# Convolution inputs by one 512-column product per weight tile, with the rounded and leftover halves of the rows side by side

## The chip, the cores and the metric

The kernel runs on one core of a Trainium2 chip as one program. The time is device microseconds of that core for one execution, from a few executions; lower is better. The engines are named as the profile names them: PE (TensorE; PEld are its weight loads, which overlap the matmuls), DVE (VectorE), ACT (ScalarE), POOL (GpSimd) and SP, which here only starts DMAs.

## The reference, cut to what matters

Two blocks of two layers each work on a sequence of 256 rows and 1024 features, all in float32. The change touches the second block, where each layer makes 2048 convolution channels from the normed rows `u` (256 x 1024):

```
z = u @ w_in                                   # its first 2048 columns are m_qk
m_qk = silu(causal_dwconv(m_qk, m_conv_w, m_conv_b))
# y[t] = w[3]*x[t] + w[2]*x[t-1] + w[1]*x[t-2] + w[0]*x[t-3] + b, for each channel
m_q, m_k = split(m_qk, 2)                      # 4 heads of 256 each; mlstm_chunkwise uses them
```

Beside it each of these layers has a sliding-window attention with 16 query heads, an mLSTM with 4 heads, two gates, and two feed-forward parts.

## The kernel before, in words

**Products.** A float32 product is made of three products in PE's `float32r` type. Each operand is split into a rounded part and what is left of it: `wh` and `wl` for weights, `xh` and `xl` for the normed and transposed rows (`[128, 8, 256]`: 8 feature tiles `kt` of 256 sequence positions). The kernel adds high x high, low x high and high x low in PSUM. Weights come in 778 units of 128 x 1024 values. SP loads a unit into `raw` (a ring of 11), ACT rounds it into `wh` (L1250, ring of 8), and DVE subtracts to make `wl` (L1475, ring of 11).

**Forms.** In the form "rows" (L1918 to L1926) a 128 x 128 tile of `xh` or `xl` is loaded into the array and 512 weight columns stream past it. In the form "features" (L1906 to L1916), which only the convolution uses, the weight tile is loaded and the 256 positions stream past it, so that channels lie on the partitions. A convolution chunk has 256 channels: two units of 4 `kt` each and two channel tiles `ct`, each into columns 0 to 255 of its own PSUM bank. That is 48 matmuls of 256 columns. Each layer has 8 chunks, so 16 chunks in all.

**After the product.** For each `ct`, ACT writes `w[3]*x + b` from the bank into `mT` (L1352), and DVE then adds the three shifted taps from the bank in place (L1711: 255, 254 and 253 columns), each waiting for the one before it. The last one frees the bank (`d_done`). A later step `conv_silu` lets ACT take a tanh (L1357) and DVE finish the silu (L1719). The matmuls that read `mT` come much later (L2026, L2027).

**Order.** All engines walk one list of steps, each in order. `weave` mixes the dense units with the side work by a table written by hand (`UNITS_AMONG_2` here). The side work between the convolution chunks is the attention. For a pair of heads, PE makes scores (L2049, L2052), DVE masks them and takes the maximum (L1806 to L1819), ACT takes the exponential (L1431, L1434), DVE makes reciprocals of the sums (L1561, L1563), ACT scales the probabilities `Pn` (L1262, semaphore `evened`), PE transposes them (L1979), ACT copies them to `PT` (L1314), and PE multiplies by the values (L2064, L2066). The chunks are numbered 0 to 7 below. Chunk 3 of each layer stands on DVE directly ahead of L1561 and L1563, as does chunk 4, and PE's next transposes wait for the `evened` that follows.

Of the kernel before, what the change touches and what calls it, by code (L numbers as in the profile page):

```python
# [8 lines left out]
F32R = mybir.dt.float32r  # L9
I32 = mybir.dt.int32  # L10
ALU = mybir.AluOpType
ACT = mybir.ActivationFunctionType
# [3 lines left out]
P = 128  # L16
S = 256
R = S // P
D = 1024
KT = D // P  # L20
# [562 lines left out]
def plan_block2(p, t_x):  # L583
# [27 lines left out]
    def convolved(i, pair):  # L611
        c = p.chunk(("w_in", [(256 * i, 256 * i + 256)]), "x", KT, 256, pair, t_x, form="features")
        p.add("conv", c=c, i=i, n=p.count("tapped", 2) - 2)
        q["conv", i] = c

    q = {}
# [20 lines left out]
    def silu(i):  # L637
        p.add("conv_silu", i=i, c=q["conv", i], n=p.count("conv"))

# [101 lines left out]
    for j in range(2):  # L741
# [5 lines left out]
        c = Step("chunk", u=u, pair=1, nth=nth)  # L747
# [114 lines left out]
def build(nc, plan, a):  # L862

    with ExitStack() as ctx:
        def sem(name):
            return ctx.enter_context(nc.semaphore(name))
# [44 lines left out]
        spread_out = sem("spread_out")  # L911
        tapped = sem("tapped")
        conv_tanh = sem("conv_tanh")
        floored = sem("floored")
# [24 lines left out]
        o = 0  # L939
        raw, end = mem.at("raw", o, [P, NR, UNIT])  # L940
        wl, o = mem.at("wl", o, [P, NR, UNIT], F32R)
        wh, o = mem.at("wh", o, [P, NH, UNIT], F32R)
        xh, o = mem.at("xh", o, [P, KT, S], F32R)
        xl, o = mem.at("xl", o, [P, KT, S], F32R)
        x, o = mem.at("x", o, [P, R, D])
# [6 lines left out]
        b = {}  # L952
# [31 lines left out]
        for n in ("dq", "dk", "dv"):  # L984
# [61 lines left out]

        split_of = {"x": (xh, xl), "oa": (b["oa_h"], b["oa_l"]), "ob": (b["ob_h"], b["ob_l"]),
                    "oc": (b["oc_h"], b["oc_l"]), "act": (b["act_h"], b["act_l"]), "hm": (b["hm_h"], b["hm_l"]),
# [16 lines left out]
        with nc.Block() as block:  # L1065
# [168 lines left out]
            def _(act):  # L1234
# [8 lines left out]
                for st in steps:  # L1243
# [102 lines left out]
                    elif k == "conv":  # L1346
                        act.wait_ge(unit_done, st.c.u + 1)
                        act.wait_ge(p_conv, 16 * (st.l + 1))
                        for ct in range(2):
                            c = 2 * st.i + ct  # L1350
                            w = b["convw"][:, c, :]
                            act.activation(b["mT"][:, c, :], DB[2 * st.c.pair + ct][:, 0:S], ACT.Identity,  # L1352
                                           scale=w[:, 3:4], bias=w[:, 4:5]).then_inc(tapped, 1)
                    elif k == "conv_silu":
                        for ct in range(2):
                            act.wait_ge(d_done[2 * st.c.pair + ct], st.c.nth + 1)
                        act.activation(b["gt"][:, st.i % 2, :, 0:256], b["mT"][:, 2 * st.i:2 * st.i + 2, :], ACT.Tanh,  # L1357
# [87 lines left out]
            def _(dve):  # L1445
                chain = [0]
                dve.memset(b["gt"][:, 0, 0, :], 0.0).then_inc(zeros, 1)

                def link(ins):
                    chain[0] += 1  # L1450
                    ins.then_inc(dve_chain, 1)
                    dve.wait_ge(dve_chain, chain[0])

# [16 lines left out]
                for st in steps:  # L1470
# [231 lines left out]
                    elif k == "conv":  # L1702
                        dve.wait_ge(unit_done, st.c.u + 1)
                        dve.wait_ge(p_conv, 16 * (st.l + 1))
                        for ct in range(2):
                            c = 2 * st.i + ct
                            bank = 2 * st.c.pair + ct
                            t, w = b["mT"][:, c, :], b["convw"][:, c, :]
                            dve.wait_ge(tapped, st.n + ct + 1)
                            for back in (1, 2, 3):  # L1710
                                ins = dve.scalar_tensor_tensor(t[:, back:S], DB[bank][:, 0:S - back],  # L1711
                                                               w[:, 3 - back:4 - back], t[:, back:S], ALU.mult, ALU.add)
                                if back < 3:
                                    link(ins)
                            ins.then_inc(d_done[bank], 1)
                    elif k == "conv_silu":
                        dve.wait_ge(conv_tanh, st.n)
                        t = b["mT"][:, 2 * st.i:2 * st.i + 2, :]
                        last = dve.scalar_tensor_tensor(t, b["gt"][:, st.i % 2, :, 0:256], 1.0, t, ALU.add, ALU.mult)  # L1719
# [137 lines left out]
            def _(pe):  # L1857
# [8 lines left out]
                for st in steps:  # L1866
# [4 lines left out]
                    if k in ("unit", "first_tile"):  # L1871
# [34 lines left out]
                        if st.form == "features":  # L1906
                            for ct in range(2):
                                out = DB[2 * st.pair + ct][:, 0:S]
                                for i in range(st.nk):
                                    kt, at = st.kt0 + i, i * st.n + ct * P  # L1910
                                    w_h, w_l = wh[:, sh, at:at + P], wl[:, sl, at:at + P]
                                    pe.matmul(out, w_h, lh[:, kt, :], start=st.first and i == 0, stop=False)  # L1912
                                    pe.matmul(out, w_h, ll[:, kt, :], start=False, stop=False)  # L1913
                                    last = pe.matmul(out, w_l, lh[:, kt, :], start=False,  # L1914
                                                     stop=st.last and i == st.nk - 1)
                            last.then_inc(unit_done, 1)  # L1916
                            continue
# [258 lines left out]
```

## Time and profile before

| | us |
|---|---|
| runs of the kernel before (3) | 2354.78 median, 2354.47 to 2356.04 |
| span of the profiled execution | 2353.8 |
| PE busy in it | 2338.4 |
| DVE busy | 1456.3 |
| ACT busy | 1236.8 |
| matmuls of the convolution form (L1912 to L1914) | 768, at 1217.7 to 1991.3 |

The span runs from the first to the last instruction of the profiled execution. No separate total is given for that execution; the median of the runs lies 1.0 us above its span. The granted clock of PE is 1.000 on average. A matmul's duration in the trace contains its way through the array, and the next one starts before it ends. What a matmul costs is therefore read from the distance between starts.

### The profile page before, as it was taken

To read this page: it belongs to the slowest core of one execution; us is meant where nothing else is said; L and a number is where in the kernel's file an instruction comes from. 1 tells how busy PE (TensorE), PEld (TensorE's weight loads), DVE (VectorE), ACT (ScalarE), POOL (GpSimd) and SP (SyncE) were. 2 spreads that over 40 slices of the span, in tenths; PEclk is the share of its full clock that TensorE was granted. 3 is DMA by queue.
4 is the path that set the end of the run, shared out by engine and by line. 5 is a ranking of instruction groups with operands and counts; after the bars stand their busy time and mean duration, and the time that the engine had idled before them with its cause. 6 is when DMAs were issued, how large, how long until landed. Compare 5 with 4: busy or idle time off the path is not lost.

```text
span 2353.8 us, 30021 instructions
## 1 busy us (share of the span) xinstructions
PE 2338.4 (99%) x11432; PEld 1945.8 (83%) x11432; DVE 1456.3 (62%) x2243; ACT 1236.8 (53%) x1910; POOL 122.4 (5%) x135
## 2 busy tenths in 40 slices
PE   9999999999999999999999999999999999999999
PEld 7788888878888888788888888888888888888887
DVE  5656775565567855565477666554755587666554
ACT  5555444445555444354467654544544478555443
POOL 0330000004300000000000000000000000000000
PEclk9999999999999999999999999999999999999999
DMA  8454456555454565555554444655555554455552
GB/s 312 159 190 165 166 206 237 187 171 178 152 197 169 184 213 186 171 191 197 169 189 154 160 152 161 217 186 178 204 191 191 175 167 153 148 174 187 175 195 106
DMA packets 118076, 427.52 MB, mean 182 GB/s; under 512 B 13616, under 2 KB 14384, under 8 KB 116912
## 3 DMA queue, kind: packets, MB, share of 16 engines
q1 hardware_dynamic: 117792, 425.56, 53.6%
q8 instruction: 92, 1.51, 0.3%
q14 instruction: 48, 0.39, 0.1%
q10 hardware_dynamic: 144, 0.07, 0.0%
HBM read 424.52 MB, written 1.05 MB: 181 GB/s over the span
## 4 chain that ended last, share of the span: by engine, by line
PE 96%; DVE 2%; DMA 1%; issue 0%; ACT 0%; POOL 0%; DVEq 0%
PE bank L1924 28%; PE bank L1926 28%; PE bank L1925 28%; PE bank L1979 4%; PE bank L1912 1%; PE bank L1913 1%; PE bank L1914 1%; DMA raw<-in_weights 1%; PE bank L2064 1%; DVE wl L1475 1%; PE bank L2026 0%; PE bank L2049 0%; PE bank L1997 0%; DVE x L1648 0%; DVE bst L1639 0%
## 5 line engine op out<-in xcount | busy, mean ns | idle before, releaser
L1250 ACT ACTIVATE wh<-raw 128x1024 fp32r<-128x1024 f32 (+1 forms) x778 | 817.0, 1053 | 901.8 <-PE bank L1926 862.4
L1475 DVE TENSOR_TENSOR wl<-raw,wh 128x1024 fp32r<-128x1024 f32 (+1 forms) x778 | 936.7, 1219 | 445.1 <-ACT wh L1250 440.3
L1924 PE MATMUL bank<-wh,xh 128*128 128x512 f32 (+1 forms) x2174 | 862.5, 397 | 5.4 <-DVE xl L1487 4.4
L1926 PE MATMUL bank<-wh,xl 128*128 128x512 f32 (+1 forms) x2174 | 846.1, 389 | 0.0
L1925 PE MATMUL bank<-wl,xh 128*128 128x512 f32 (+1 forms) x2174 | 844.3, 388 | 0.0
L1924 PEld LDWEIGHTS bank<-wh,xh 128*128 128x128 f32 x2174 | 408.7, 188 | 87.0 <-issue 7.8
L1926 PEld LDWEIGHTS bank<-wh,xl 128*128 128x128 f32 x2174 | 408.2, 188 | 84.6
L1925 PEld LDWEIGHTS bank<-wl,xh 128*128 128x128 f32 x2174 | 409.2, 188 | 77.8
L1924 PE MATMUL bank<-wh,act_h 128*128 128x512 f32 x528 | 207.4, 393 | 0.0
L1926 PE MATMUL bank<-wh,act_l 128*128 128x512 f32 x528 | 205.9, 390 | 0.0
L1925 PE MATMUL bank<-wl,act_h 128*128 128x512 f32 x528 | 205.7, 390 | 0.0
L1926 PEld LDWEIGHTS bank<-wh,act_l 128*128 128x128 f32 x528 | 99.1, 188 | 20.9
L1924 PEld LDWEIGHTS bank<-wh,act_h 128*128 128x128 f32 x528 | 99.2, 188 | 20.0
L1925 PEld LDWEIGHTS bank<-wl,act_h 128*128 128x128 f32 x528 | 99.2, 188 | 19.8
L1851 DVE SCALAR_TENSOR_TENSOR ffn_a<-bank,scr,ffn_s 128x256 f32<-128x256 f32 (+1 forms) x88 | 37.8, 468 | 71.2 <-ACT ffn_s L1441 71.2
L1912 PE MATMUL bank<-xh,wh 128*128 128x256 f32 x256 | 74.6, 291 | 0.0
L1913 PE MATMUL bank<-xl,wh 128*128 128x256 f32 x256 | 72.5, 283 | 0.0
L1914 PE MATMUL bank<-xh,wl 128*128 128x256 f32 x256 | 72.5, 283 | 0.0
L1253 ACT ACTIVATE xh<-bank 128x512 fp32r<-128x512 f32 x64 | 35.1, 590 | 59.3 <-PE bank L1979 59.0
L1185 POOL TENSOR_TENSOR scr<-scr 128x1 f32<-128x1 f32 x12 | 10.2, 850 | 1039.2 <-DVE scr L1646 686.7
L1711 DVE SCALAR_TENSOR_TENSOR mT<-bank,convw,mT 128x255 f32<-128x255 f32 (+2 forms) x96 | 44.8, 480 | 17.4 <-ACT mT L1352 15.0
L1188 POOL TENSOR_TENSOR scr<-scr 128x2 f32<-128x2 f32 x6 | 9.7, 1610 | 852.5 <-DVE scr L1676 852.5
(350 smaller groups left out, 2178.2 us busy)
## 6 DMA issues: line engine op xcount, KB each, us to landing
raw<-in_weights SPq DMA_DIRECT2D x760, 512.0 KB, 3.3
raw<-in_weights SPq DMA_DIRECT2D x16, 384.0 KB, 3.0
ln<-in_ln SPq DMA_DIRECT2D x4, 1024.0 KB, 6.2
bias<-in_bias SPq DMA_DIRECT2D x2, 1024.0 KB, 10.7
b_merge<-in_b_merge SPq DMA_DIRECT2D x2, 1024.0 KB, 5.5
gain<-in_gain_ffn SPq DMA_DIRECT2D x4, 512.0 KB, 3.8
decay<-in_decay SPq DMA_DIRECT2D x2, 768.0 KB, 12.5
x<-in_x SPq DMA_DIRECT2D x2, 512.0 KB, 5.5
```

What stands on the lines that cost most here:

```text
L1250: act.activation(wh[:, u % NH, 0:used(u)], raw[:, u % NR, 0:used(u)], ACT.Copy).then_inc(hi_done, 1)
L1253: act.activation(split_of[st.dst][0][:, st.kg:st.kg + 4, st.tile * P:st.tile * P + P], TB[st.t % 2][:, :].rearrange("p (k n) -> p k n", k= ...
L1475: dve.tensor_tensor(wl[:, u % NR, 0:used(u)], raw[:, u % NR, 0:used(u)], wh[:, u % NH, 0:used(u)].bitcast(F32), ALU.subtract).then_inc(lo_ ...
L1711: ins = dve.scalar_tensor_tensor(t[:, back:S], DB[bank][:, 0:S - back], w[:, 3 - back:4 - back], t[:, back:S], ALU.mult, ALU.add)
L1851: ins = dve.scalar_tensor_tensor(dst, up, root[:, r:r + 1], s_in, ALU.mult, ALU.mult)
L1912: pe.matmul(out, w_h, lh[:, kt, :], start=st.first and i == 0, stop=False)
L1913: pe.matmul(out, w_h, ll[:, kt, :], start=False, stop=False)
L1914: last = pe.matmul(out, w_l, lh[:, kt, :], start=False, stop=st.last and i == st.nk - 1)
L1924: pe.matmul(out, h, w_h, start=st.first and i == 0, stop=False)
L1925: pe.matmul(out, h, w_l, start=False, stop=False)
L1926: last = pe.matmul(out, lo, w_h, start=False, stop=st.last and i == st.nk - 1)
L1979: last = pe.transpose(bank[:, i * P:(i + 1) * P], piece, ident[:, :])
```

## The change

The rounded and the leftover rows become one buffer `xs` of `[128, 8, 2, 256]`, so that for one `kt` both lie side by side. In the convolution form one matmul with `wh` streams all 512 columns: the rounded half lands in columns 0 to 255 of the bank, the leftover half in columns 256 to 511. The product with `wl` still streams the 256 rounded columns. ACT copies the right half of the bank to SBUF (into `gt`). DVE adds the left half to it, which frees the bank, then makes the first tap with the bias from SBUF, and then the three other taps, also from SBUF, taking turns between the two channel tiles. The other forms use the same values at other addresses. The table `UNITS_AMONG_2` is not touched.

```diff
@@ memory @@
-        xh, o = mem.at("xh", o, [P, KT, S], F32R)
-        xl, o = mem.at("xl", o, [P, KT, S], F32R)
+        xs, o = mem.at("xs", o, [P, KT, 2, S], F32R)
@@ ScalarE @@
                     elif k == "conv":
                         act.wait_ge(unit_done, st.c.u + 1)
-                        act.wait_ge(p_conv, 16 * (st.l + 1))
+                        if st.i >= 2:
+                            act.wait_ge(tapped, st.m - 4)
                         for ct in range(2):
-                            c = 2 * st.i + ct
-                            w = b["convw"][:, c, :]
-                            act.activation(b["mT"][:, c, :], DB[2 * st.c.pair + ct][:, 0:S], ACT.Identity,
-                                           scale=w[:, 3:4], bias=w[:, 4:5]).then_inc(tapped, 1)
+                            act.activation(b["gt"][:, st.i % 2, ct, 256:512], DB[2 * st.c.pair + ct][:, S:2 * S], ACT.Copy)                               .then_inc(halved, 1)
                     elif k == "conv_silu":
-                        for ct in range(2):
-                            act.wait_ge(d_done[2 * st.c.pair + ct], st.c.nth + 1)
+                        act.wait_ge(tapped, st.m)
@@ VectorE @@
+                        made = [b["gt"][:, st.i % 2, ct, 256:512] for ct in range(2)]
+                        taps = [(b["mT"][:, 2 * st.i + ct, :], b["convw"][:, 2 * st.i + ct, :]) for ct in range(2)]
                         for ct in range(2):
-                            dve.wait_ge(tapped, st.n + ct + 1)
-                            for back in (1, 2, 3):
-                                ins = dve.scalar_tensor_tensor(t[:, back:S], DB[bank][:, 0:S - back],
-                                                               w[:, 3 - back:4 - back], t[:, back:S], ALU.mult, ALU.add)
+                            bank = 2 * st.c.pair + ct
+                            dve.wait_ge(halved, st.m - 1 + ct)
+                            dve.tensor_tensor(made[ct], DB[bank][:, 0:S], made[ct], ALU.add)\
+                               .then_inc(d_done[bank], 1)
+                        for ct, (t, w) in enumerate(taps):
+                            dve.wait_ge(d_done[2 * st.c.pair + ct], st.c.nth + 1)
+                            then(dve.tensor_scalar(t, made[ct], w[:, 3:4], w[:, 4:5], ALU.mult, ALU.add))
+                        for back in (1, 2, 3):
+                            dve.wait_ge(dve_chain, chain[0])
+                            for ct, (t, w) in enumerate(taps):
+                                ins = dve.scalar_tensor_tensor(t[:, back:S], made[ct][:, 0:S - back], w[:, 3 - back:4 - back],
+                                                               t[:, back:S], ALU.mult, ALU.add)
@@ TensorE, form "features" @@
-                                    pe.matmul(out, w_h, lh[:, kt, :], start=st.first and i == 0, stop=False)
-                                    pe.matmul(out, w_h, ll[:, kt, :], start=False, stop=False)
-                                    last = pe.matmul(out, w_l, lh[:, kt, :], start=False,
+                                    pe.matmul(bank[:, :], wh[:, sh, at:at + P], xs[:, kt, :, :].rearrange("p a s -> p (a s)"),
+                                              start=st.first and i == 0, stop=False)
+                                    last = pe.matmul(bank[:, 0:S], wl[:, sl, at:at + P], lh[:, kt, :], start=False,
                                                      stop=st.last and i == st.nk - 1)
```

VectorE at chunk 3 of the first of these layers, before. The names are the buffers, and the brackets name the semaphores waited for:

```order
L1711 SCALAR_TENSOR_TENSOR mT<-bank,convw,mT 128x255 [waits tapped,p_conv,unit_done]
L1711 SCALAR_TENSOR_TENSOR mT<-bank,convw,mT 128x254 [waits dve_chain]
L1711 SCALAR_TENSOR_TENSOR mT<-bank,convw,mT 128x253 [waits dve_chain]
L1711 SCALAR_TENSOR_TENSOR mT<-bank,convw,mT 128x255 [waits tapped]
L1711 SCALAR_TENSOR_TENSOR mT<-bank,convw,mT 128x254 [waits dve_chain]
L1711 SCALAR_TENSOR_TENSOR mT<-bank,convw,mT 128x253 [waits dve_chain]
L1719 SCALAR_TENSOR_TENSOR mT<-gt,mT 128x512 [waits conv_tanh]
L1561 TENSOR_TENSOR scr<-sc_119 128x4 [waits soft]
L1563 RECIPROCAL scr<-scr 128x4 [waits dve_chain]
```

The same place on VectorE in the changed kernel:

```order
L1710 TENSOR_TENSOR gt<-bank,gt 128x256 [waits halved,p_conv,unit_done]
L1710 TENSOR_TENSOR gt<-bank,gt 128x256 [waits halved]
L1714 TENSOR_SCALAR mT<-gt,convw 128x256 [waits d_done2]
L1714 TENSOR_SCALAR mT<-gt,convw 128x256 [waits d_done3]
L1718 SCALAR_TENSOR_TENSOR mT<-gt,convw,mT 128x255 [waits dve_chain]
L1718 SCALAR_TENSOR_TENSOR mT<-gt,convw,mT 128x255
L1718 SCALAR_TENSOR_TENSOR mT<-gt,convw,mT 128x254 [waits dve_chain]
L1718 SCALAR_TENSOR_TENSOR mT<-gt,convw,mT 128x254
L1718 SCALAR_TENSOR_TENSOR mT<-gt,convw,mT 128x253 [waits dve_chain]
L1718 SCALAR_TENSOR_TENSOR mT<-gt,convw,mT 128x253
L1728 SCALAR_TENSOR_TENSOR mT<-gt,mT 128x512 [waits tapped,conv_tanh]
L1561 TENSOR_TENSOR scr<-sc_118 128x4 [waits soft]
```

Six operations became ten ahead of the same L1561. What follows stands in the same order as before.

ScalarE at the same place, before:

```order
L1250 ACTIVATE wh<-raw 128x1024 [waits unit_done,w_loaded4]
L1352 ACTIVATE mT<-bank,convw 128x256 [waits p_conv,unit_done]
L1352 ACTIVATE mT<-bank,convw 128x256
L1357 ACTIVATE gt<-mT 128x2x256 [waits d_done1,d_done0]
L1262 ACTIVATE Pn<-Pn,scr 128x256 [waits shares]
```

And now:

```order
L1250 ACTIVATE wh<-raw 128x1024 [waits unit_done,w_loaded4]
L1351 ACTIVATE gt<-bank 128x256 [waits tapped,unit_done]
L1351 ACTIVATE gt<-bank 128x256
L1354 ACTIVATE gt<-mT 128x2x256 [waits tapped]
L1262 ACTIVATE Pn<-Pn,scr 128x256 [waits shares]
```

ScalarE keeps the number and the order of its operations; the two from the bank are plain copies now, and they wait for the taps of the chunk two before as well.

## Rows read from the trace of the kernel before

**Rows 1.** The page: busy time, chain that ended last, costliest group of ACT.

```profile
PE 2338.4 (99%) x11432; PEld 1945.8 (83%) x11432; DVE 1456.3 (62%) x2243; ACT 1236.8 (53%) x1910; POOL 122.4 (5%) x135
...
PE 96%; DVE 2%; DMA 1%; issue 0%; ACT 0%; POOL 0%; DVEq 0%
...
L1250 ACT ACTIVATE wh<-raw 128x1024 fp32r<-128x1024 f32 (+1 forms) x778 | 817.0, 1053 | 901.8 <-PE bank L1926 862.4
```

**Rows 2.** Timeline of PE: start us, us, engine, line, operation [idle before].

```profile
1199.96 0.39 PE L1924 MATMUL bank<-wh,xh 128*128 128x512 f32 x1
...
1214.24 0.39 PE L1924 MATMUL bank<-wh,xh 128*128 128x512 f32 x1
...
1217.66 0.28 PE L1912 MATMUL bank<-xh,wh 128*128 128x256 f32 x1
...
1220.18 0.28 PE L1912 MATMUL bank<-xh,wh 128*128 128x256 f32 x1
```

**Rows 3.** Groups by form, DVE: busy us, mean ns | idle before.

```profile
L1711 DVE SCALAR_TENSOR_TENSOR mT<-bank,convw,mT 128x255 f32<-128x255 f32 x32 | 15.3, 478 | 15.1 <-ACT mT L1352 15.0
...
L1853 DVE TENSOR_TENSOR ffn_a<-ffn_s,bank 128x256 f32<-128x256 f32 x44 | 16.6, 418 | 38.3 <-ACT ffn_s L1441 38.3
...
L1795 DVE SCALAR_TENSOR_TENSOR mo<-m_o,scr,mo 128x256 f32<-128x256 f32 x16 | 6.5, 477 | 0.1
...
L1578 DVE TENSOR_SCALAR Pn<-Pn,scr 128x256 f32<-128x256 f32 x8 | 2.8, 348 | 0.0
```

**Rows 4.** Groups by form, ACT.

```profile
L1352 ACT ACTIVATE mT<-bank,convw 128x256 f32<-128x256 f32 x32 | 16.1, 552 | 0.0
...
L1363 ACT ACTIVATE aqk<-bank 128x256 f32<-128x256 f32 x4 | 1.5, 371 | 0.0
```

**Rows 5.** Timeline of DVE, chunks 0 to 3 of the first layer.

```profile
1228.19 2.93 DVE L1711 SCALAR_TENSOR_TENSOR mT<-bank,convw,mT 128x255 f32<-128x255 f32 x6
1231.04 2.35 DVE L1475 TENSOR_TENSOR wl<-raw,wh 128x1024 fp32r<-128x1024 f32 x2
1233.40 2.94 DVE L1711 SCALAR_TENSOR_TENSOR mT<-bank,convw,mT 128x255 f32<-128x255 f32 x6
...
1253.13 2.94 DVE L1711 SCALAR_TENSOR_TENSOR mT<-bank,convw,mT 128x255 f32<-128x255 f32 x6 [0.89 <-ACT mT L1352]
...
1259.51 2.94 DVE L1711 SCALAR_TENSOR_TENSOR mT<-bank,convw,mT 128x255 f32<-128x255 f32 x6 [0.56 <-ACT mT L1352]
...
1263.15 0.18 DVE L1563 RECIPROCAL scr<-scr 128x4 f32<-128x4 f32 x1
```

**Rows 6.** Timeline of ACT, same stretch.

```profile
1241.24 0.60 ACT L1431 ACTIVATE Pn<-Pn,sc 128x256 f32<-128x256 f32 x1 [2.04 <-DVE sc L1819]
...
1251.48 1.06 ACT L1250 ACTIVATE wh<-raw 128x1024 fp32r<-128x1024 f32 x1 [0.49 <-PE bank L1914]
...
1263.36 1.50 ACT L1262 ACTIVATE Pn<-Pn,scr 128x256 f32<-128x256 f32 x4 [3.01 <-DVE scr L1563]
```

**Rows 7.** Timeline of PEld, the transposes behind chunk 3.

```profile
1264.70 0.48 PEld L1979 LDWEIGHTS bank<-ident,Pn 128*128 128x128 f32 x3
```

**Rows 8.** Timelines of DVE, ACT and PEld, chunk 4 to the last chunk.

```profile
1280.94 2.94 DVE L1711 SCALAR_TENSOR_TENSOR mT<-bank,convw,mT 128x255 f32<-128x255 f32 x6 [0.49 <-ACT mT L1352]
...
1327.99 1.29 DVE L1752 SCALAR_TENSOR_TENSOR mo<-mo,gain 128x512 f32<-128x512 f32 x2 [0.48 <-ACT mo L1381]
...
1330.21 1.50 ACT L1262 ACTIVATE Pn<-Pn,scr 128x256 f32<-128x256 f32 x4 [1.32 <-DVE scr L1563]
...
1333.22 0.48 PEld L1979 LDWEIGHTS bank<-ident,Pn 128*128 128x128 f32 x3
```

**Rows 9.** Timeline of DVE, chunk 3 of the second layer.

```profile
1936.44 2.94 DVE L1711 SCALAR_TENSOR_TENSOR mT<-bank,convw,mT 128x255 f32<-128x255 f32 x6 [0.57 <-ACT mT L1352]
```

**Rows 10.** Timeline of PE at the kernel's start.

```profile
9.20 0.99 PE L1886 MATMUL bank<-wh,xh 128*128 128x512 f32 x1
...
11.49 0.39 PE L1924 MATMUL bank<-wh,xh 128*128 128x512 f32 x1
```

More of the change, by code:

```diff
@@ L612, in convolved @@
         c = p.chunk(("w_in", [(256 * i, 256 * i + 256)]), "x", KT, 256, pair, t_x, form="features")
-        p.add("conv", c=c, i=i, n=p.count("tapped", 2) - 2)
-        q["conv", i] = c
+        q["conv", i] = p.count("tapped", 2)
+        p.add("conv", c=c, i=i, m=q["conv", i])
     q = {}
@@ L637, in silu @@
     def silu(i):
-        p.add("conv_silu", i=i, c=q["conv", i], n=p.count("conv"))
+        p.add("conv_silu", i=i, m=q["conv", i], n=p.count("conv"))
     for i in range(4):
@@ L912, in build @@
         tapped = sem("tapped")
+        halved = sem("halved")
         conv_tanh = sem("conv_tanh")
@@ L1045, in build @@
         lamv, root, vsum, halves = scr[:, 204:212], scr[:, 212:216], scr[:, 216:218], scr[:, 218:220]
-        split_of = {"x": (xh, xl), "oa": (b["oa_h"], b["oa_l"]), "ob": (b["ob_h"], b["ob_l"]),
+        split_of = {"x": (xs[:, :, 0, :], xs[:, :, 1, :]), "oa": (b["oa_h"], b["oa_l"]), "ob": (b["ob_h"], b["ob_l"]),
                     "oc": (b["oc_h"], b["oc_l"]), "act": (b["act_h"], b["act_l"]), "hm": (b["hm_h"], b["hm_l"]),
@@ L1447, in _, with then, link @@
                 dve.memset(b["gt"][:, 0, 0, :], 0.0).then_inc(zeros, 1)
-                def link(ins):
+                def then(ins):
                     chain[0] += 1
                     ins.then_inc(dve_chain, 1)
+                def link(ins):
+                    then(ins)
                     dve.wait_ge(dve_chain, chain[0])
@@ L1704, in _ @@
                         dve.wait_ge(p_conv, 16 * (st.l + 1))
+                        made = [b["gt"][:, st.i % 2, ct, 256:512] for ct in range(2)]
+                        taps = [(b["mT"][:, 2 * st.i + ct, :], b["convw"][:, 2 * st.i + ct, :]) for ct in range(2)]
                         for ct in range(2):
-                            c = 2 * st.i + ct
                             bank = 2 * st.c.pair + ct
-                            t, w = b["mT"][:, c, :], b["convw"][:, c, :]
-                            dve.wait_ge(tapped, st.n + ct + 1)
-                            for back in (1, 2, 3):
-                                ins = dve.scalar_tensor_tensor(t[:, back:S], DB[bank][:, 0:S - back],
-                                                               w[:, 3 - back:4 - back], t[:, back:S], ALU.mult, ALU.add)
+                            dve.wait_ge(halved, st.m - 1 + ct)
[9 more added lines that the diff above has]
+                                                               t[:, back:S], ALU.mult, ALU.add)
                                 if back < 3:
-                                    link(ins)
-                            ins.then_inc(d_done[bank], 1)
+                                    then(ins)
+                                else:
+                                    ins.then_inc(tapped, 1)
                     elif k == "conv_silu":
                         dve.wait_ge(conv_tanh, st.n)
+                        dve.wait_ge(tapped, st.m)
                         t = b["mT"][:, 2 * st.i:2 * st.i + 2, :]
@@ L1907, in _ @@
                             for ct in range(2):
-                                out = DB[2 * st.pair + ct][:, 0:S]
+                                bank = DB[2 * st.pair + ct]
                                 for i in range(st.nk):
                                     kt, at = st.kt0 + i, i * st.n + ct * P
-                                    w_h, w_l = wh[:, sh, at:at + P], wl[:, sl, at:at + P]
-                                    pe.matmul(out, w_h, lh[:, kt, :], start=st.first and i == 0, stop=False)
-                                    pe.matmul(out, w_h, ll[:, kt, :], start=False, stop=False)
-                                    last = pe.matmul(out, w_l, lh[:, kt, :], start=False,
+                                    pe.matmul(bank[:, :], wh[:, sh, at:at + P], xs[:, kt, :, :].rearrange("p a s -> p (a s)"),
+                                              start=st.first and i == 0, stop=False)
+                                    last = pe.matmul(bank[:, 0:S], wl[:, sl, at:at + P], lh[:, kt, :], start=False,
                                                      stop=st.last and i == st.nk - 1)
```

## The prediction

> **What bounds the kernel now.** I read the page first. PE is busy for 99% of the span, and the chain that ended last runs on PE for 96% of it [rows 1]. ACT's largest group, the rounding of the weights, idles 862.4 us in wait for PE: the weight rings are full, so ACT and DVE are ahead with weights [rows 1]. In these terms the time is the sum of PE's spacings, and a microsecond of DVE costs nothing, unless PE waits for just that piece of work. Second comes the spacing. In PE's timeline 63 matmuls of 512 columns lie between the starts 1199.96 and 1214.24, so 226.7 ns each. 21 of 256 columns lie between 1217.66 and 1220.18, so 120.0 ns each [rows 2]. Their difference, 106.7 ns, is 256 columns at 2.4 GHz; what is left is 13.3 ns for each matmul, whatever its width. Third, the timelines of DVE and ACT between the chunks, because there the side work is handed round, with PE at its end.
>
> **PE: two matmuls become one.** A weight tile cost 3 x 120.0 = 360.0 ns and now costs 226.7 + 120.0 = 346.7 ns. The 768 matmuls of the form are 256 such triples: 256 x 13.3 = 3.4 us less, or 0.21 us a chunk and 0.85 us for four chunks. The columns streamed are the same number.
>
> The Trainium skill ("TensorE: Matmul & The Clock Gate", Back-to-back issue gap) gives a warm spacing of N/2.4 + 2.5 ns. By it the merge would save 256 x 2.5 ns, an estimate of 0.6 us. The rows of this kernel, whose matmuls each bring a weight load, show 13.3 ns, so the sum goes by them.
>
> **ACT.** Two operations of 552 ns become copies like L1363, 371 ns [rows 4]. DVE can begin about 0.18 us sooner where it waits for the first of them. Nothing else on ACT gets longer.
>
> **DVE: six operations become ten.** Before, a chunk takes 1231.04 - 1228.19 = 2.85 us from its start to the next operation's [rows 5]. A successor that waits for nothing starts about 0.1 us before its predecessor ends (two of 1.23 in 2.35), and one that waits for it some 0.03 us after it ends [rows 5]. Now:
> - two adds from bank and SBUF, as L1853, 418 ns: 0.42 + 0.33 = 0.75
> - two first taps from SBUF, as L1578, 348 ns: 2 x 0.25 = 0.50
> - three pairs of taps from SBUF alone, as L1795, 477 ns against 478 from the bank [rows 3]: (0.51 + 0.39) x 3 = 2.70
>
> That makes 3.95 us to the next start, **1.10 us more for each chunk**. Bounds: with the taps at the pace of the add (418 ns) the surplus is 0.74; if each of the ten waited for the one before, 1.8. I take 1.10; every part has a row of its shape and its places of operands.
>
> The Trainium skill ("VectorE: DVE Perf Modes", Rules for kernel authors) advises copying a matmul's output from PSUM to SBUF first when many operations follow, which is what is done here. By its cycle table (58 against 120 fixed cycles) six taps would be cheaper by an estimated 0.39 us. In the rows a tap costs the same from either place.
>
> **Does PE see it?** Weights no: ACT waits for PE, not the other way. The banks no: they come free after the two adds rather than after six taps, so earlier. The side work yes. In the first of these layers:
> - Chunks 0 and 1 run on DVE with no idle time before them [rows 5]. Masks and maxima behind them come 2.2 us late.
> - ACT was already idle 2.04 us for those (L1431) [rows 6], so it is 2.2 late too, and works without a gap up to 1251.48, where 0.49 of idle time and the lost overlap of 0.1 take 0.6 off. Less the 0.18 of its own quicker copies, chunk 2 starts on DVE 1.4 late. (DVE's own 0.89 of idle time [rows 5] gives the same.)
> - Chunk 2 makes it 2.5. The 0.56 idle before chunk 3 [rows 5] takes 0.65: 1.85. Chunk 3 makes it 2.95.
> - Right behind it come the reciprocals at 1263.15 [rows 5], for which ACT was waiting 3.01 us, and then L1262, four scalings in 1.50 us [rows 6]. The first head's two end near 1264.16, and PE loads for that head's transposes at 1264.70 [rows 7]. The margin is 0.54 at most; with the handing over I take 0.35.
>
> So PE reaches these transposes 2.95 - 0.35 = 2.6 us later than before, although its own matmuls would have been there 0.85 earlier: it stands still for about 3.45 us where it never stopped. Queued behind are a whole unit and all else on PE, since it works in order. With d for the surplus this is 4d - 1.8.
>
> From there chunk 4 is paced by PE again, since ACT's gap before it ended with PE. Then the same builds up: chunks 4 to 7 each add 1.10 - 0.18, and only the 0.48 idle before L1752 takes some back [rows 8]. The next close place is 1333.22: L1262 starts at 1330.21 [rows 8], its first two end near 1331.01, which leaves 2.0 after handing over. (2.6 - 0.2) + 3.7 - 0.5 - 2.0 = 3.6 us late. I take 3.5 for a layer; all its savings on matmuls are in that, because the lateness is measured against the old clock. The second layer has the same gap before its chunk 3 (0.57) [rows 9].
>
> **Sum.** The profiled span is 2353.8, and the median of the runs is 1.0 above it. 2353.8 + 2 x 3.5 + 1.0 = 2361.8, and as the steps are good to some tenths I say **2361.5 us**. Without DVE's part it would be 2354.8 - 3.4 = 2351.4.
>
> **Rivals.**
> - *A, the cover holds.* DVE idles for 38% of the span, and the delay never reaches PE. For it: PE idled for almost nothing, and ACT waits for PE on weights. Against: the 0.54 at 1264.70, and the chain of waits with only 1.5 us of idle time in it. Time 2351.4. It decides if d is under 0.45.
> - *B, the taps are cheaper from SBUF.* d = 0.74: the first stall puts PE 1.2 behind, and by the layer's end (8d - 5.2) it is 0.7 behind. Time 2354.8 + 1.4 = 2356.2. The row of L1795 speaks against it. The skill's rule named above would put it here.
> - *C, the clock falls as well.* PE has run without a gap. At the start, after waiting, a matmul of 512 columns shows 0.99 us and later 0.39 [rows 10], so PE there came up from the lower of its levels (1.2 GHz). If a stall of 3.4 us has that effect, some microseconds run at half speed, 2 to 4 us of time for each layer: 2366 to 2369. Against it: the stall is short beside the start.
> - *D, the merge gives more than the spacing shows,* say through quieter SBUF reads. Nothing in the rows speaks for it: under 2350.
>
> **How the numbers follow.** About 0.2%, 4.7 us, is what a measurement can tell. Forecast 0.50, with its own range 2358 to 2365; A 0.17; B 0.20; C 0.08; D 0.05. Faster by over 0.2% (under 2350.1) needs D: 0.05, with a little of A 0.07. Slower by over 0.2% (over 2359.5): nearly nine tenths of the forecast, all of C, a little of B: 0.54. Within: 0.39. The range from A to the edge of C is 2351 to 2366.
>
> **What would show it.** Right: PE's timeline with spacings of 0.227 and 0.120 in turn; L1710, L1714 and L1718 taking 3.9 to 4.0 us a chunk with no idle time ahead of chunk 3; PEld waiting about 3.4 us at the L1979 behind chunk 3 in both layers, ended by ACT's `Pn`, and a second wait of 1 to 2 us in all between there and the last transposes. Wrong: PE without idle time there (A), a chunk under 3.7 us (B), a granted clock below 1.00 after the stall (C), or a matmul spacing other than 0.227 and 0.120 (D).

## The result, and the profile after

| | us, median | lowest to highest | profiled run, span | clock |
|---|---|---|---|---|
| before | 2354.78 | 2354.47 to 2356.04 | 2353.8 | 1.000 |
| after | 2366.17 | 2363.91 to 2367.04 | 2363.5 | 0.999 |

The change makes the kernel 0.45% slower: ratio 1.0045, 95% interval 1.0034 to 1.0056. The forecast was 2361.5 us and the direction was right. The median lies 0.2 us over the upper end of the whole range (2366), and 1.2 us over the forecast's own range (2358 to 2365).

The page after, line for line with [rows 1]:

```profile
PE 2340.2 (99%) x11176; PEld 1930.9 (82%) x11176; DVE 1474.6 (62%) x2307; ACT 1229.8 (52%) x1910; POOL 122.4 (5%) x135
...
PE 86%; DVE 9%; ACT 3%; issue 2%; DMA 1%; POOL 0%; DVEq 0%; ACTq 0%
...
L1250 ACT ACTIVATE wh<-raw 128x1024 fp32r<-128x1024 f32 (+1 forms) x778 | 816.1, 1052 | 892.7 <-PE bank L1934 854.7
```

PE's share of the span still reads 99%. What changed is the chain that ended last: 96% PE before, now 86% with 9% DVE and 3% ACT. VectorE was no busier than before in percent, and yet the end now hangs on it for a while. The groups that answer to [rows 3, 4], busy us and mean ns:

```profile
L1718 DVE SCALAR_TENSOR_TENSOR mT<-gt,convw,mT 128x255 f32<-128x255 f32 x32 | 14.1, 481 | 0.6
...
L1710 DVE TENSOR_TENSOR gt<-bank,gt 128x256 f32<-128x256 f32 x32 | 12.0, 417 | 10.7 <-ACT gt L1351 10.5
...
L1714 DVE TENSOR_SCALAR mT<-gt,convw 128x256 f32<-128x256 f32 x32 | 11.6, 405 | 0.0
...
L1351 ACT ACTIVATE gt<-bank 128x256 f32<-128x256 f32 x32 | 10.2, 373 | 0.0
```

Three of the four are as the forecast priced them. The first tap takes 405 ns and not 348. The timeline of VectorE, for [rows 5]:

```profile
1227.38 0.75 DVE L1710 TENSOR_TENSOR gt<-bank,gt 128x256 f32<-128x256 f32 x2
1228.05 0.73 DVE L1714 TENSOR_SCALAR mT<-gt,convw 128x256 f32<-128x256 f32 x2
1228.81 2.71 DVE L1718 SCALAR_TENSOR_TENSOR mT<-gt,convw,mT 128x255 f32<-128x255 f32 x6
1231.43 2.36 DVE L1475 TENSOR_TENSOR wl<-raw,wh 128x1024 fp32r<-128x1024 f32 x2
...
1253.84 0.76 DVE L1710 TENSOR_TENSOR gt<-bank,gt 128x256 f32<-128x256 f32 x2
...
1260.77 0.74 DVE L1710 TENSOR_TENSOR gt<-bank,gt 128x256 f32<-128x256 f32 x2
...
1265.60 0.18 DVE L1563 RECIPROCAL scr<-scr 128x4 f32<-128x4 f32 x1
```

A chunk now takes 1231.43 - 1227.38 = 4.05 us against 2.85: the surplus is 1.20, forecast 1.10. The brackets of idle time before chunks 2 and 3 (0.89 and 0.56) are gone, and the reciprocal stands at 1265.60 where it stood at 1263.15. What waits for it, on ScalarE and then on TensorE's weight load, in the first layer and (last row) the second:

```profile
1265.81 1.49 ACT L1262 ACTIVATE Pn<-Pn,scr 128x256 f32<-128x256 f32 x4 [7.05 <-DVE scr L1563]
...
1266.72 0.31 PEld L1987 LDWEIGHTS bank<-ident,Pn 128*128 128x128 f32 x3 [3.29 <-issue]
...
1302.38 0.31 PEld L1987 LDWEIGHTS bank<-ident,Pn 128*128 128x128 f32 x3 [0.52 <-issue]
...
1309.13 0.19 PEld L1920 LDWEIGHTS bank<-xs,wh 128*128 128x128 f32 x1 [0.65 <-ACT mo L1378]
...
1336.35 0.31 PEld L1987 LDWEIGHTS bank<-ident,Pn 128*128 128x128 f32 x3 [0.93 <-issue]
...
1948.40 0.49 PEld L1987 LDWEIGHTS bank<-ident,Pn 128*128 128x128 f32 x3 [3.29 <-issue]
```

ScalarE waited 3.01 us there before and 7.05 now [rows 6]. TensorE had no idle time at the row of [rows 7]; now it stands 3.29 us. After the second layer's stall something else shows. PE's timeline:

```profile
1948.43 0.86 PE L1987 MATMUL bank<-ident,Pn 128*128 128x128 f32 x3 [2.89 <-ACT Pn L1262]
1948.94 0.78 PE L1932 MATMUL bank<-wh,xs 128*128 128x512 f32 x1
1949.52 0.63 PE L1933 MATMUL bank<-wl,xs 128*128 128x512 f32 x1
1949.94 0.63 PE L1934 MATMUL bank<-wh,xs 128*128 128x512 f32 x1
...
1952.21 0.39 PE L1934 MATMUL bank<-wh,xs 128*128 128x512 f32 x1
```

and in stretches of 5 us (busy us and instructions of PE, PEld, DVE, ACT and POOL, then PE's granted clock, the DMA share and GB/s):

```profile
1940.00:1945.00 5.00, 5.00 (x23) 4.11 (x23) 4.93 (x10) 0.44 (x1) 0.00 (x0) 1.00 0.37 129
1945.00:1950.00 5.00, 2.11 (x9) 1.52 (x8) 4.76 (x19) 2.25 (x7) 0.00 (x0) 0.85 0.42 150
1950.00:1955.00 5.00, 5.00 (x21) 4.06 (x20) 2.79 (x4) 5.00 (x12) 0.00 (x0) 0.81 0.13 34
1955.00:1960.00 5.00, 5.00 (x34) 3.75 (x33) 2.99 (x14) 3.67 (x9) 0.00 (x0) 1.00 0.53 179
```

Mean clocks of 0.85 and 0.81 in two stretches of 5 us come to 3.4 us at half clock, the lower of TensorE's levels (1.2 GHz): a matmul of 512 columns shows 0.63 us and starts 0.42 to 0.43 after the last, where 0.39 and 0.227 are usual. This is rival C. It had a chance of 0.08.

To see where time is lost the two traces are laid side by side. For each unit of weights I take the start of its first product on TensorE, in this trace less in that of before. How much this lateness grows from a layer's first convolution product to its end is what the layer costs. The last column is what of it grew while the clock was low. In us:

| kernel | surplus of a chunk | PEld wait behind chunk 3 | layer 1 | layer 2 | of it at half clock, layer 1, layer 2 |
|---|---|---|---|---|---|
| after | 1.20 | 3.29, 3.29 | +4.24 | +5.80 | 0, 1.60 |
| product only | 0 | none | -0.98 | -0.99 | 0, 0 |
| adds and taps only | as after | 2.93, 2.92 | +5.90 | +5.91 | 1.58, 1.59 |
| taps held back | moved | none | +1.39 | +1.39 | 0, 0 |
| matmuls in the stall | as after | filled | +4.19 | +4.19 | 0, 0 |
| held, not over the gate | moved | none | -0.98 | -0.99 | 0, 0 |
| one add more | 0.33 | none | +0.01 | -0.01 | 0, 0 |
| three adds more | 1.00 | 1.85, 1.88 | +3.43 | +3.43 | 0, 0 |
| first tap, one operand | 1.08 | 2.91, 2.90 | +4.87 | +4.85 | 1.58, 1.59 |
| wide, then narrow | moved | none | -1.10 | -1.11 | 0, 0 |
| held again | moved | none | -0.97 | -0.99 | 0, 0 |

"Moved" means that the taps stand elsewhere on VectorE, "filled" that other matmuls stand in the wait.

Without the falls the two layers of a kernel agree to 0.1 us. Outside the conv layers the traces drift apart, the kernels being the same there: by up to 1.3 us before the first layer and 0.5 between the two, for moments by more. So single spans are compared by the table and not by their difference. With 4.2 to 4.3 us a layer and one or two falls of the clock at 1.6, the change costs 10.0 to 11.8 us. The medians differ by 11.4. One run of after was traced, with one fall. The three longest of its five runs have a mean clock of 0.998 and the two shortest 0.999, which fits a second fall in the three but does not show it.

### The profile page after: what moved, and what is told of

The parts are those of the page before. It is cut to its first block, busy times and chain, and to the rows that moved or that the text cites. A ratio compares the mean times of both kernels' runs of the same rounds, so it can differ in the third digit from the quotient of the medians.

```text
span 2363.5 us, 29569 instructions
## 1 busy us (share of the span) xinstructions
PE 2340.2 (99%) x11176; PEld 1930.9 (82%) x11176; DVE 1474.6 (62%) x2307; ACT 1229.8 (52%) x1910; POOL 122.4 (5%) x135
## 4 chain that ended last, share of the span: by engine, by line
PE 86%; DVE 9%; ACT 3%; issue 2%; DMA 1%; POOL 0%; DVEq 0%; ACTq 0%
PE bank L1932 26%; PE bank L1934 26%; PE bank L1933 26%; PE bank L1987 4%; DVE wl L1475 2%; DVE mT L1718 2%; ACT Pn L1428 1%; ACT wh L1250 1%; DMA raw<-in_weights 1%; DVE gt L1710 0%; DVE mT L1714 0%; PE bank L2034 0%; PE bank L2005 0%; DVE mT L1728 0%; DVE Pn L1815 0%
## 5 line engine op out<-in xcount | busy, mean ns | idle before, releaser
L1932 PE MATMUL bank<-wh,xs 128*128 128x512 f32 (+1 forms) x2174 | 862.5, 397 | 5.1 <-DVE xs L1487 4.2
L1934 PE MATMUL bank<-wh,xs 128*128 128x512 f32 (+1 forms) x2174 | 845.7, 389 | 0.0
L1933 PE MATMUL bank<-wl,xs 128*128 128x512 f32 (+1 forms) x2174 | 843.8, 388 | 0.0
L1932 PEld LDWEIGHTS bank<-wh,xs 128*128 128x128 f32 x2174 | 408.8, 188 | 87.4 <-issue 7.8
L1934 PEld LDWEIGHTS bank<-wh,xs 128*128 128x128 f32 x2174 | 408.3, 188 | 85.1
L1933 PEld LDWEIGHTS bank<-wl,xs 128*128 128x128 f32 x2174 | 409.3, 188 | 78.2
L1920 PE MATMUL bank<-xs,wh 128*128 128x512 f32 x256 | 93.5, 406 | 0.7 <-issue 0.7
L1922 PE MATMUL bank<-xs,wl 128*128 128x256 f32 x256 | 71.7, 280 | 0.0
L1253 ACT ACTIVATE xs<-bank 128x512 fp32r<-128x512 f32 x64 | 35.1, 591 | 57.7 <-PE bank L1987 57.5
L1920 PEld LDWEIGHTS bank<-xs,wh 128*128 128x128 f32 x256 | 48.1, 188 | 13.0 <-ACT mo L1378 1.2
L1487 DVE TENSOR_TENSOR act_l<-bank,act_h 128x512 fp32r<-128x512 f32 x66 | 45.6, 691 | 12.3 <-ACT act_h L1271 11.9
```

Of the source, the lines that this page charges most:

```text
L1253: act.activation(split_of[st.dst][0][:, st.kg:st.kg + 4, st.tile * P:st.tile * P + P], TB[st.t % 2][:, :].rearrange("p (k n) -> p k n", k= ...
L1487: ins = dve.tensor_tensor(lo, bank, h.bitcast(F32), ALU.subtract)
L1920: pe.matmul(bank[:, :], wh[:, sh, at:at + P], xs[:, kt, :, :].rearrange("p a s -> p (a s)"), start=st.first and i == 0, stop=False)
L1922: last = pe.matmul(bank[:, 0:S], wl[:, sl, at:at + P], lh[:, kt, :], start=False, stop=st.last and i == st.nk - 1)
L1932: pe.matmul(out, h, w_h, start=st.first and i == 0, stop=False)
L1933: pe.matmul(out, h, w_l, start=False, stop=False)
```

## The experiments

**Product only.** Before, with after's buffer and product, and nothing else:

```
-  pe.matmul(out, w_h, lh[:, kt, :], ...)
-  pe.matmul(out, w_h, ll[:, kt, :], ...)
-  last = pe.matmul(out, w_l, lh[:, kt, :], ...)
+  pe.matmul(bank[:, :], w_h, xs[:, kt, :, :], ...)
+  last = pe.matmul(bank[:, 0:S], w_l, lh[:, kt, :], ...)
```

> Only TensorE's part of the change: the rounded and the leftover rows lie side by side and one product of 512 columns streams them, but ScalarE and VectorE read the left half of the bank alone, by the instructions of the kernel before. Left out of the computation: the product of the rounded weights with the leftover rows, which stands in the right half and is never added. Theory (VectorE's longer chain is what costs, the product itself gives 13.3 ns for each matmul it saves): 256 x 13.3 ns = 3.4 us less than the kernel before, about 2351.4 us, and TensorE waits no more than 0.5 us at the transposes behind chunk 3 of a layer, which it reaches 0.85 us sooner against a cover of 0.35. Rival (the merged product itself costs something, through the doubled width of the write into the bank or the interleaved rows in SBUF): at or over the 2354.8 us of before, with spacings other than 0.227 and 0.120 us. Rival by the Trainium skill's gap of 2.5 ns: 2354.2 us.

Measured: 2353.53 us against 2355.43 of before in the same comparison, ratio 0.9994 (0.9985 to 1.0003), an interval that takes in no change. The size rests on the traces: the table says 0.98 and 0.99 us a layer, so the product saves 2.0 us, not 3.4. One stretch of PE's timeline, from the first product to the next other operation:

```profile
1950.68 0.48 PE L1910 MATMUL bank<-xs,wh 128*128 128x512 f32 x1
1951.00 0.28 PE L1912 MATMUL bank<-xs,wl 128*128 128x256 f32 x1
1951.12 0.40 PE L1910 MATMUL bank<-xs,wh 128*128 128x512 f32 x1
...
1953.24 0.40 PE L1910 MATMUL bank<-xs,wh 128*128 128x512 f32 x1
1953.47 0.28 PE L1912 MATMUL bank<-xs,wl 128*128 128x256 f32 x1
1953.59 0.38 PE L1977 MATMUL bank<-ident,Pn 128*128 128x128 f32 x2
```

Eight pairs take 2.91 us, and the eight triples of before at this place 2.96 (1953.00 to 1955.96). The steady pair takes 350 ns (medians 233 and 117) and not 346.7, and the first wide product of a stretch, started behind transposes, takes 320 ns to the next start where the first narrow one took 200. All 26 such stretches, from their first start to that of their last product, take 90.95 us before and 88.87 here, 2.1 us less. The stalls are not TensorE's doing: there are none here.

**Adds and taps only.** After, with the leftover product as a matmul of its own again:

```
-  pe.matmul(bank[:, :], w_h, xs[:, kt, :, :], ...)
+  if st.first and i == 0:  pe.matmul(bank[:, :], w_h, xs[:, kt, :, :], ...)
+  else:
+      pe.matmul(bank[:, 0:S], w_h, lh[:, kt, :], ...)
+      pe.matmul(bank[:, S:2 * S], w_h, ll[:, kt, :], ...)
```

> Only the part of VectorE and ScalarE: the leftover product goes into the right half of the bank by a matmul of its own of 256 columns (except the first tile of each bank, 32 of 256, which stays merged), so TensorE has 224 of its 256 saved matmuls back. Everything else is as in the changed kernel. Theory (in the conv stage TensorE's time is set by VectorE's chain at two or three places, so its own savings before each of them are lost anyway): the stalls get shorter by what TensorE takes longer, 0.7 us for the first four chunks of a layer; the time is that of the changed kernel plus 0 to 1.5 us, 2366 to 2367.7. Rival (the terms add up: VectorE's part costs a fixed sum and the merged product saves 3.0 us of it): 2366.2 + 3.0 = 2369.2 us.

Measured: 2366.92 us, ratio 1.0045 (1.0032 to 1.0057), that of the changed kernel. Net of the clock a layer costs 4.32 against 4.24 and 4.20. So TensorE's microsecond a layer is lost in the waits, as the first theory has it. The stall is 2.93 where it was 3.29:

```profile
1267.17 0.31 PEld L1991 LDWEIGHTS bank<-ident,Pn 128*128 128x128 f32 x3 [2.93 <-issue]
```

The medians alone would not tell, since what there is to add has shrunk from 3.0 to 1.8; the table does.

**Taps held back.** After, with another order on VectorE:

```
+  def late(...): the two first taps and the three pairs, unchanged
+  held.append(late)
   # at the head of each step:
+  if held and (prior == "aa_s" or st.kind == "conv_silu" and st.i == 7):
+      while held: held.pop(0)()
   # and at the head of each conv step, before its adds, the same
```

> The changed kernel with another order on VectorE and nothing else: at a chunk it issues the two adds alone, which free the banks, and holds back the eight operations of the four taps until the row maxima of the next attention step are out (or until the next chunk's adds or the last silu). Instructions, operands and their number are the same. Theory (the loss is the lateness of maxima and reciprocals behind the taps): no wait of TensorE over 0.5 us behind chunk 3 of either layer, clock 1.000, time 2351.4 to 2354, so about 12 us less than the changed kernel and at or below the kernel before. Rival (the loss is not one of order: the added work of VectorE, or its reads of the same SBUF beside TensorE's, slows the stage as a whole): over 2362 us in spite of the order. Second rival: the held taps now delay the weights' subtraction behind them, so that TensorE waits for a weight instead of a probability: 2355 to 2362.

Measured: 2357.99 us, ratio 1.0012 (1.0003 to 1.0021). Neither 2351 to 2354 nor over 2362. The stalls behind chunk 3 are gone in both layers. The loss that is left stands at one place, rows of VectorE and PEld:

```profile
1325.75 1.29 DVE L1770 SCALAR_TENSOR_TENSOR mo<-mo,gain 128x512 f32<-128x512 f32 x2 [2.75 <-ACT mo L1378]
1326.96 0.73 DVE L1722 TENSOR_SCALAR mT<-gt,convw 128x256 f32<-128x256 f32 x2
...
1331.93 0.18 DVE L1568 RECIPROCAL scr<-scr 128x4 f32<-128x4 f32 x1
...
1333.06 0.31 PEld L1996 LDWEIGHTS bank<-ident,Pn 128*128 128x128 f32 x3 [2.12 <-issue]
```

I had put the last chunk's taps behind the gate, for which VectorE first idles 2.75 us. The second rival named the right range and the wrong reason: it is a probability that comes late, not a weight.

**Matmuls in the stall.** After, with ten matmuls ahead of the wait:

```
+  if st.of == "aa" and st.h == 2:
+      for _ in range(10): pe.matmul(bank[:, 0:P], ident, ident, start=True, stop=True)
```

> The changed kernel with ten matmuls of 128 x 128 ahead of TensorE's wait for the probabilities behind chunk 3 of each layer; they write into the left quarter of the bank that the transposes then fill anew, and nobody reads what they make. They take part of a wait of 3.3 us that is there in any case. Theory (part of the loss is the half clock of 3.4 us that follows the second layer's stall): TensorE's idle time there falls below 3 us, the clock stays at 1.000 through both layers, and the time is 1.5 to 3.2 us below the changed kernel, 2363 to 2364.7. Rival (the half clock after the stall costs nothing of its own, since the time behind it is made up at the next wait, or it comes all the same): 2366.2 us, no change.

Measured: 2363.51 us, ratio 1.0035 (1.0023 to 1.0048), 2.4 us below the changed kernel by the ratios, 2.7 by the medians. The two intervals overlap, so the times alone do not tell the kernels apart. Weight loads of the added matmuls, and of the transposes that wait:

```profile
1264.16 2.42 PEld L1974 LDWEIGHTS bank<-ident 128*128 128x128 f32 x20
...
1267.35 0.31 PEld L1990 LDWEIGHTS bank<-ident,Pn 128*128 128x128 f32 x3 [0.77 <-ACT Pn L1262]
```

The wait for the probabilities ends no earlier: TensorE goes on 2.6 us late in either kernel. Only what TensorE does meanwhile has changed, the clock stays at 1.00 in both layers, and each costs 4.19. In this trace of after the second layer had its fall behind the same stall, and cost 1.6 more. So the half clock has a price of its own. That the added matmuls kept it away is likely and not certain: the first layer of after had a stall of 3.29 us without a fall.

**Held, not over the gate.** The flush before the last `conv_silu` becomes one before `m_gate`:

```
-  if held and (prior == "aa_s" or st.kind == "conv_silu" and st.i == 7):
+  if held and (prior == "aa_s" or st.kind == "m_gate"):
```

> The kernel with the taps held back, with one difference: the taps of a layer's last chunk run ahead of the gate step (m_gate) on VectorE and not behind it, where VectorE had 2.75 us of idle time just before. In the run with the taps held back TensorE lost 1.9 us at the transposes behind chunk 7 and 0.45 at the next ones, in each layer, all of it behind those late taps. Theory (what is left of the loss is that one place): 2 x 2.35 = 4.7 us less than that run, about 2353.3 us, no wait of TensorE over 1 us in the stage, and 2 us below the kernel before, which is what the merged product saved by itself. Rival (the taps ahead of the gate delay the gate's product, its sum or the weights' subtraction instead): 2355.5 to 2358.

Measured: 2352.83 us, before 2354.80, ratio 0.9992 (0.9983 to 1.0001). The place that cost 1.9 and 0.45 us a layer now reads:

```profile
1322.88 0.73 DVE L1722 TENSOR_SCALAR mT<-gt,convw 128x256 f32<-128x256 f32 x2
1323.65 2.70 DVE L1726 SCALAR_TENSOR_TENSOR mT<-gt,convw,mT 128x255 f32<-128x255 f32 x6
1326.27 1.29 DVE L1770 SCALAR_TENSOR_TENSOR mo<-mo,gain 128x512 f32<-128x512 f32 x2
...
1328.26 0.18 DVE L1568 RECIPROCAL scr<-scr 128x4 f32<-128x4 f32 x1
```

The reciprocal is 3.67 us earlier, the gate's product 0.52 later, and no one waits for that. The layers come out as in the product-only kernel, -0.98 and -0.99. Every instruction of the change is there, and all that it cost is gone by order alone.

**One add more, three adds more.** Before, with adds that nobody reads ahead of each chunk's taps (`range(ct)` for one, `range(1 + ct)` for three):

```
+  for j in range(ct):
+      chain[0] += 1
+      dve.tensor_tensor(b["gt"][:, st.i % 2, j, 256:512], DB[bank][:, 0:S], x[:, j, 0:S], ALU.add)...
```

> The kernel before with one add more on VectorE for each chunk (bank and SBUF into SBUF, 128 x 256, ahead of the taps; nobody reads its result), nothing else. It makes a chunk 0.33 to 0.42 us longer. Theory (VectorE's surplus reaches TensorE only beyond the slack on the way: four times the surplus less 0.6, 0.65 and 0.35 at the transposes behind chunk 3, four times the surplus less 2.5 at the next place): 4 x 0.35 - 1.6 is below nothing, so no change: within 1 us of the kernel before, 2354.5 to 2356.5. Rival (a microsecond more on VectorE in this stage costs a share of itself everywhere, by the ratio of the changed kernel: 8.4 us for 16 x 1.2): 16 x 0.35 x 0.44 = 2.5 us, 2357.9.

Measured: 2355.03 against 2354.80, ratio 1.0001 (0.9992 to 1.0010). A chunk is 0.33 us longer, the reciprocal comes 0.35 us later by TensorE's clock, and the layers cost nothing. The proportional rival, 2.5 us, is out.

> The kernel before with three such adds for each chunk, nothing else: 1.0 to 1.2 us more on VectorE, which is the surplus of the change, while TensorE's product, ScalarE's steps and the place of the first tap stay as before. Theory (the loss is VectorE's added time alone): TensorE waits about 2.6 us behind chunk 3 of each layer and stands 4 to 4.5 us later at a layer's end, the clock may fall once or twice for 1.4 us each: 2363 to 2367 us. Rival (the loss needs what else the change does: the taps' start tied to both halves, ScalarE's copies, the first tap waiting for the add): under 2359 us.

Measured: 2361.35 us, ratio 1.0029 (1.0018 to 1.0041), below the 2363 to 2367 I expected, and over the rival's 2359. The surplus was 1.00 and not up to 1.2, and the clock did not fall behind chunk 3. Rows of DVE and PEld:

```profile
1227.45 0.42 DVE L1712 TENSOR_TENSOR gt<-bank,x 128x256 f32<-128x256 f32 x1
1227.79 1.51 DVE L1715 SCALAR_TENSOR_TENSOR mT<-bank,convw,mT 128x255 f32<-128x255 f32 x3
...
1231.30 2.35 DVE L1475 TENSOR_TENSOR wl<-raw,wh 128x1024 fp32r<-128x1024 f32 x2
...
1266.16 0.31 PEld L1983 LDWEIGHTS bank<-ident,Pn 128*128 128x128 f32 x3 [1.85 <-issue]
```

Nothing of the change is in this kernel but VectorE's time, and it has the same stall at the same place. A third of that time is free, the whole is not.

**First tap with one operand.** After, with the bias left out:

```
-  dve.tensor_scalar(t, made[ct], w[:, 3:4], w[:, 4:5], ALU.mult, ALU.add)
+  dve.tensor_scalar(t, made[ct], w[:, 3:4], 0.0, ALU.mult, ALU.add)
```

> The changed kernel with the convolution's bias left out: the first tap multiplies by one column of numbers and adds the constant zero. This asks what makes the first tap take 405 ns where the row of the nearest shape had 348. Theory (the second operand that is a column costs 57 ns): the first tap takes about 348 ns, a chunk 3.95 us from its start to the next operation's, and the time is 1 to 2 us below the changed kernel. Rival (the shape or where it stands decides): 405 ns and 4.05 us as in the changed kernel.

Measured, one run: 2364.38 us, and for the group:

```profile
L1714 DVE TENSOR_SCALAR mT<-gt,convw 128x256 f32<-128x256 f32 x32 | 9.7, 345 | 0.0
```

The adding of the constant zero is still there, so 60 ns of the 405 are the second operand that is a column. A chunk takes 0.12 us less, and a layer net of the clock 3.3 us where it was 4.2: eight times the 0.12, in the one execution that there is.

**Wide, then narrow.** The last version, with the four wide products of a half ahead of the four narrow ones (two loops over `i` in place of one).

> The kernel of the run with the taps held back, but not over the gate, and in it one more thing: in a unit's half, TensorE's four products of 512 columns come first and the four of 256 columns after them, where they stood in turn. In turn a pair took 233 + 117 = 350 ns in the steady part, against 226.7 and 120.0 for runs of one width. Theory (the change of width costs 3.3 ns a pair): pairs of 347 ns, 256 x 3.3 ns = 0.8 us less, about 2352.0 us. Rival (the 350 ns come from what is streamed: 512 columns that lie as two halves): spacing of the wide ones stays near 233 ns, the sum at 350, no change from 2352.8.

Measured: 2353.24 us, beside 2353.37 of the next kernel in the same comparison. Wide after wide starts at 234 ns, as in turn (233), and the trace has 0.12 us less a layer than that of the next kernel, where the theory asks for 0.4: the rival holds. Why a wide product costs 7 ns more here than the 226.7 of [rows 2] stays open.

**Held again.**

> The same kernel as the run with the taps held back but not over the gate, run again, because its interval against the kernel before (0.9983 to 1.0001) just takes in no change. Theory (the merged product gives 2 x 1.0 us once nothing else waits): 2352.5 to 2353.2 us, 2 us below the kernel before in the same comparison. Rival (the 2 us were scatter): within 1 us of the kernel before.

Measured: 2353.37 us, before 2355.34, ratio 0.9991 (0.9982 to 1.0000). That and its first comparison give 2.0 us each by the medians, and so does the table. One interval just takes in no change and the other ends at it. It is the best version of this study, by an amount at the edge of what can be measured.

## Why the prediction was right, and where it was off

- *What bounds the kernel: right.* VectorE's surplus counts only where TensorE waits for that piece of work. 0.33 us a chunk costs nothing and 1.00 costs 3.4 us a layer, by themselves. The sum had the path right: chunk 3's taps, the reciprocals, ScalarE's scaling, TensorE's transposes.
- *The product, 3.4 us saved: wrong size, 2.0 to 2.1.* The fixed 13.3 ns were read off stretches of one width each [rows 2]. In the new product the wide one starts the next after 233 instead of 226.7, and behind other work both start slower. The Trainium skill ("TensorE: Matmul & The Clock Gate", Back-to-back issue gap) has 2.5 ns for each, an estimate of 0.6 us; the runs lie between its figure and mine. For the forecast it did not matter, since the waits swallow it, as the step said and the run with adds and taps only shows. For rival A it did: with the cover held the time is 2353, not 2351.4.
- *The surplus, 1.10: 1.20.* The adds (417 ns) and taps (481) came out as their rows. The cheaper SBUF reads of the Trainium skill ("VectorE: DVE Perf Modes", the cycle table in its section on the TRN2 errata) show nowhere: a tap takes 478 ns from the bank and 481 from SBUF. The first tap was priced by L1578, a TENSOR_SCALAR of the same shape but with one column as operand and nothing added. The second one costs 60 ns more.
- *TensorE late by 2.6 us behind chunk 3: measured 2.66.* This is luck: two errors cancel. With 1.20 the formula gives 3.0. By TensorE's clock the reciprocal at 1265.60 comes 3.26 late and TensorE 2.66, so the margin that I took as 0.35 is 0.6. The three adds say the same: the formula gives 4 x 1.00 - 1.6 = 2.4, and the reciprocal comes 2.6 late and TensorE 2.0.
- *3.5 us a layer: 4.2.* This term of the sum was too small. I had two places where TensorE waits. There are more behind the first: 0.52 at 1302.38, 0.65 at 1309.13 (the gate's sum), 0.93 at 1336.35, and some 0.5 at the next transposes, 2.6 in all where I had 1 to 2. Once the slack is used up, each further chunk's surplus comes through: the run with one operand, next to after, shows it with a factor of eight. The run with three adds does not lie on the same line (3.4 us at a surplus of 1.00, where one operand has 3.3 at 1.08), so the slack is not the same in every kernel.
- *Rival C, 0.08: it came, on top of the forecast and not in its place.* The sum had the clock at nothing. TensorE stood 2.9 us or more behind chunk 3 at six places of the runs (after, adds and taps only, one operand), and the clock fell at five of them, for 1.6 us each, where C had 2 to 4. Where it stood 1.85 to 2.12, at four places, it did not. I had counted the stall as short beside the start's. The trace of before did hold a nearer case that I passed over: at 994.45 PEld stood 2.95 us and the clock stayed at 1.00, but at this same place it fell in five traces of this study. One trace could not have settled it, and it should have had more than 0.08.
- *The 4.7 us over the forecast.* 2361.8 was rounded to 2361.5, 0.3. Two layers at 0.7 more are 1.4, a fall of the clock 1.6: with one fall 3.3, with two 4.9. The 4.7 of the median lies between.
- *Outside the span* nothing was missed. The runs of after, and those of before whose spans are on record, are 1.7 to 1.9 us longer than their own spans. The 1.0 was the distance of before's median from the span of one execution that was 0.8 longer than the median's, and the sum 2353.8 + 1.0 rightly starts at the median.

## What to carry to other kernels

When a stage has an engine at 99%, find the last wait on each path into it and its slack in microseconds; work added to another engine is free up to that and, by the runs here, comes through beyond it, in the end once for each chunk. When such work has grown, first look whether someone waits for what is queued behind it, and put only the part that others need (here the two adds that free the banks) in front. And price a stall on TensorE at more than its length where it has run without a gap: here five of six stalls of 2.9 us and more behind chunk 3 cost 1.6 us on top.

## What the runs showed of the hardware

- A VectorE TENSOR_SCALAR of 128 x 256 in f32 takes 405 ns with two columns as operands and 345 with one and a constant.
- With ten matmuls of 128 x 128 (20 records, 2.4 us) in a wait of 3.3 us TensorE's clock stayed at 1.00 in both layers of the one trace. Behind the six unfilled waits of 2.9 to 3.3 us at this place it fell five times. The median was 2.7 us lower though the probabilities came no sooner, with intervals that overlap.
- A fall of the clock does not always cost. In the run with the taps held, not over the gate, PEld stood as in before, and the clock was low behind it:

```profile
993.40 0.19 PEld L1941 LDWEIGHTS bank<-wh,xs 128*128 128x128 f32 x1 [2.94 <-issue]
```

```profile
990.00:995.00 5.00, 2.46 (x10) 1.72 (x9) 5.00 (x6) 3.13 (x7) 0.00 (x0) 0.96 0.75 282
995.00:1000.00 5.00, 5.00 (x17) 3.92 (x17) 4.76 (x10) 0.00 (x0) 0.99 (x1) 0.70 0.00 0
```

The lateness grew by less than 0.1 us across it. In before TensorE waits 1.20 us once more at 1002.34, and in this trace that wait is gone: the slower stretch took its place. Behind chunk 3 only shorter waits follow, and the fall costs 1.6.
- The clock can fall behind shorter waits too: in the run with one add more it did at 508.6, where PEld had stood 1.33 and 0.71 us in the microseconds before (and 1.67 at 499.56), and that cost 1.6 us in a stage that the change does not touch. So the length of one wait does not tell when it falls.
